# The update of x in a two-block transformer kernel: gain product in its own buffer, block 1 in two parts, last mean on VectorE

## The reference

```python
merged = concatenate([rms_norm(y_ssm, g_ssm), rms_norm(y_attn, g_attn)])
h = h + rms_norm(merged @ w_out, g_post_mix)       # the update of x
hn = rms_norm(h, g_pre_ffn)
gu = hn @ w_gate_up
ff = (silu(gu[..., :D_FF]) * gu[..., D_FF:]) @ w_down
return h + rms_norm(ff, g_post_ffn)                # the tail
```

## Time and profile before

| | us (the clock: a share) |
|---|---|
| median of 3 runs | 791.45 |
| lowest, highest run | 790.4, 792.85 |
| the profiled execution, its whole time | 792.52 |
| the profiled execution, span from first to last instruction | 790.7 |
| TensorE busy in the span | 775.4 |
| VectorE, ScalarE, GpSimd busy | 516.2, 405.2, 233.4 |
| TensorE's granted clock, mean, share of full speed | 0.998 |

### The profile page before, as it was taken

One profiled execution on the slowest core, in us unless ns is written; L12 is line 12 of the kernel. 1 busy time (PEld: TensorE's weight loads), 2 busy tenths in 40 slices (PEclk: granted clock), 3 DMA queues, 4 the chain that ended last, 5 costly groups with the idle time before them and its releaser, 6 DMA issues.

```text
span 790.7 us, 12717 instructions
## 1 busy us (share of the span) xinstructions
PE 775.4 (98%) x5139; PEld 678.8 (86%) x5139; DVE 516.2 (65%) x759; ACT 405.2 (51%) x649; POOL 233.4 (30%) x186
## 2 busy tenths in 40 slices
PE   8999999999999999999999999999999999999996
PEld 7889988999889889987778888989887888888885
DVE  4846884764547657866557965785678676777453
ACT  5644357534565545344335545717766555556341
POOL 3031896570742000036009910126002111011010
PEclk9999999999999999999999999999999999999999
DMA  9897996387621554655544556440363656654651
GB/s 229 200 240 203 219 221 172 84 196 170 164 81 53 188 173 147 214 165 146 159 143 148 183 200 188 134 134 2 133 220 121 198 183 212 186 183 167 222 177 54
DMA packets 78110, 130.72 MB, mean 165 GB/s; under 512 B 4447, under 2 KB 28243, under 8 KB 77923
## 3 DMA queue, kind: packets, MB, share of 16 engines
q1 hardware_dynamic: 76608, 124.96, 54.7%
q0 software_dynamic: 1200, 4.83, 1.9%
q10 hardware_dynamic: 242, 0.11, 0.1%
HBM read 128.82 MB, written 1.06 MB: 164 GB/s over the span
## 4 chain that ended last, share of the span: by engine, by line
PE 88%; DVE 4%; DMA 3%; ACT 3%; issue 1%; POOL 0%; DVEq 0%; SPq 0%; POOLq 0%; ACTq 0%
PE ps L1521 13%; PE ps L1525 13%; PE ps L1529 13%; PE ps L1561 10%; PE ps L1540 6%; PE ps L1544 6%; PE ps L1548 6%; PE ps L1565 5%; DMA stage<-in_even_w_in 3%; PE ps L1632 2%; PE ps L1651 2%; DVE w_lo L925 1%; ACT w_hi L636 1%; PE ps L1664 1%; PE ps L1663 1%
## 5 line engine op out<-in xcount | busy, mean ns | idle before, releaser
L925 DVE TENSOR_TENSOR w_lo<-stage,w_hi 128x1024 fp32r<-128x1024 f32 x226 | 299.6, 1346 | 161.9 <-ACT w_hi L636 161.3
L636 ACT ACTIVATE w_hi<-stage 128x1024 fp32r<-128x1024 f32 x232 | 242.2, 1061 | 240.0 <-PE ps L1529 106.6
L1521 PE MATMUL ps<-w_hi,act_t 128*128 128x512 f32 (+1 forms) x376 | 102.7, 395 | 4.0 <-issue 1.8
L1529 PE MATMUL ps<-w_lo,act_t 128*128 128x512 f32 (+1 forms) x376 | 98.8, 385 | 0.1
L1561 PE MATMUL ps<-act_t,w_hi 128*128 128x512 f32 x352 | 88.3, 393 | 0.7 <-DVE act_t L962 0.7
L1521 PEld LDWEIGHTS ps<-w_hi,act_t 128*128 128x128 f32 x376 | 67.9, 188 | 17.5 <-issue 2.8
L1529 PEld LDWEIGHTS ps<-w_lo,act_t 128*128 128x128 f32 x376 | 69.6, 188 | 14.8 <-DVE w_lo L925 0.5
L1525 PE MATMUL ps<-w_hi,act_t 128*128 128x512 f32 (+1 forms) x312 | 81.6, 384 | 0.0
L1561 PEld LDWEIGHTS ps<-act_t,w_hi 128*128 128x128 f32 x352 | 63.3, 189 | 12.2 <-issue 0.9
L1525 PEld LDWEIGHTS ps<-w_hi,act_t 128*128 128x128 f32 x312 | 57.6, 188 | 13.9 <-issue 2.0
L1540 PE MATMUL ps<-act_t,w_hi 128*128 128x256 f32 x416 | 58.9, 284 | 0.9 <-ACT w_hi L636 0.9
(11 more groups left out here) (364 smaller groups left out, 1197.2 us busy)
## 6 DMA issues: line engine op xcount, KB each, us to landing
stage<-in_even_w_in SPq DMA_DIRECT2D x64, 512.0 KB, 5.9
stage<-in_odd_w_in SPq DMA_DIRECT2D x48, 512.0 KB, 4.1
stage<-in_w_gate_up SPq DMA_DIRECT2D x44, 512.0 KB, 4.6
stage<-in_w_down SPq DMA_DIRECT2D x22, 512.0 KB, 4.1
stage<-in_even_w_out SPq DMA_DIRECT2D x16, 512.0 KB, 3.8
stage<-in_odd_w_out SPq DMA_DIRECT2D x16, 512.0 KB, 4.4
stage<-in_w_in SPq DMA_DIRECT2D x10, 512.0 KB, 4.5
stage<-in_w_out SPq DMA_DIRECT2D x8, 512.0 KB, 4.7
```

The source lines that it names most:

```text
L636: nc.scalar.activation(w_hi[:, u % RING, :], stage[:, u % RING, :], ACT.Copy).then_inc(hi_ready, 1)
L925: nc.vector.tensor_tensor(w_lo[:, u % RING, :], stage[:, u % RING, :], w_hi[:, u % RING, :].bitcast(F32), ALU.subtract).then_inc(lo_ready, 1)
L1521: mm(out[:, b, :], a_hi(k)[:, tok[b]], hi[:, i, :], start=(k == 0), stop=False)
L1529: ins = mm(out[:, b, :], a_hi(k)[:, tok[b]], lo[:, i, :], start=False, stop=(k == k_tiles - 1))
```

## The change

In words:

- `mix_gain(1, b)` writes to a new buffer `gained`, laid over a part of the work area that is no longer in use, and waits only for VectorE's own sum. `x_add(1, b)` reads `gained`.
- `mix_gain(1, 1)` moves ahead of `x_add(0, 0)`.
- `x_add(0, 1)` is made in two parts of 256 channels, each counting `x_ready` up; TensorE waits for the second part before tile 2 of block 1, and ScalarE for a count one higher.
- In the tail, VectorE adds the two halves' sums and epsilon (one instruction a block), and GpSimd only takes the power. So that the sums are means already, ScalarE's squares are scaled: those of half 0 by 1024 to the power -1/2, those of half 1 by `rstd_mean`, the factor times the same number, which VectorE makes once behind `spread`. ScalarE waits for it (`mean_ready`). The diff in full stands below.

```diff
@@ -181,7 +181,7 @@
         COL_LIM = COL_LRE + ST
         COL_FINAL = COL_LIM + ST
         sumsq, sumsq_b, rstd = sb("sumsq", [P, 18]), sb("sumsq_b", [P, 18]), sb("rstd", [P, 18])
-        rstd_in, rstd_in_q = sb("rstd_in", [P, NB]), sb("rstd_in_q", [P, NB])
+        rstd_in, rstd_in_q, rstd_mean = sb("rstd_in", [P, NB]), sb("rstd_in_q", [P, NB]), sb("rstd_mean", [P, NB])
         ones, diag = sb("ones", [P, P]), sb("diag", [P, NB, P])
         rstd_row, rstd_row_q = sb("rstd_row", [P, S]), sb("rstd_row_q", [P, S])
         neg_half, half_pi = sb("neg_half", [P, 8]), sb("half_pi", [P, 1])
@@ -236,6 +236,7 @@
         ssm_a, ssm_b = over("ssm_a", 8192, [P, CT, 2, 4, NC]), over("ssm_b", 10240, [P, CT, 2, 4, NC])
         y_ssm = [ssm_b[:, ct, 0].rearrange("p q n -> p (q n)") for ct in range(CT)]
         ssm_out, gate_z = over("ssm_out", 1024, [P, NB, 512]), over("gate_z", 2048, [P, NB, 512])
+        gained = over("gained", 8192, [P, NB, 512])
         rope_tmp = over("rope_tmp", 7168, [P, 768])
         ff_hi, ff_lo = over("ff_hi", 0, [P, KF, S], F32R), over("ff_lo", 5632, [P, KF, S], F32R)
         down_out, down_junk = (big[:, i * 2048:(i + 1) * 2048].rearrange("p (b n) -> p b n", b=NB) for i in range(2))
@@ -277,7 +278,7 @@
         b_pow_ready, c_pow_ready, lag_done, lag_copied, lag_ready, fade_ready = (sem(n) for n in ("b_pow_ready", "c_pow_ready", "lag_done", "lag_copied", "lag_ready", "fade_ready"))
         gelu_hi_ready, gelu_ready, gelu_lo_ready = sem("gelu_hi_ready"), sem("gelu_ready"), sem("gelu_lo_ready")
         rope_q_ready, rope_k_ready, k_out, qk_turned, qk_ready = (sem(n) for n in ("rope_q_ready", "rope_k_ready", "k_out", "qk_turned", "qk_ready"))
-        ret_stats = sem("ret_stats")
+        ret_stats, mean_ready = sem("ret_stats"), sem("mean_ready")
         sink_sum, sink_exped, y_attn_ready = sem("sink_sum"), sem("sink_exped"), sem("y_attn_ready")
         sig_ready, ssm_out_ready = sem("sig_ready"), sem("ssm_out_ready")
         ff_raw_ready, silu_ready, ff_ready, ff_hi_ready, ff_lo_ready, ff_part = sem("ff_raw_ready"), sem("silu_ready"), sem("ff_ready"), sem("ff_hi_ready"), sem("ff_lo_ready"), sem("ff_part")
@@ -617,10 +618,8 @@
             nc.gpsimd.tensor_tensor(down_out[:, :, 0:512], down_out[:, :, 0:512], row_b[:, 0:512].unsqueeze(1).to_broadcast([P, NB, 512]), ALU.mult).then_inc(down_scaled, 1)
             for b in range(NB):
                 c = slice(16 + b, 17 + b)
-                pool.wait_ge(block_squared, b + 1)
-                then(nc.gpsimd.tensor_tensor(sumsq[:, c], sumsq[:, c], sumsq_b[:, c], ALU.add))
-                then(nc.gpsimd.tensor_scalar(rstd[:, c], sumsq[:, c], 1.0 / D, EPS, ALU.mult, ALU.add))
-                nc.gpsimd.tensor_tensor(rstd[:, c], rstd[:, c], neg_half[:, 0:1], ALU.pow).then_inc(rstd_ready, 1)
+                pool.wait_ge(block_mean, NB + b + 1)
+                nc.gpsimd.tensor_tensor(rstd[:, c], sumsq[:, c], neg_half[:, 0:1], ALU.pow).then_inc(rstd_ready, 1)
 
 
         @block.scalar
@@ -879,7 +878,7 @@
                     nc.scalar.activation(junk[:, b, half], mixed[:, b, half], ACT.Square, scale=D**-0.5, accum_out=(sumsq, sumsq_b)[c][:, 12 + b:13 + b]).then_inc(squared, 1)
             ahead(("mix_ssm", 1))
             hi_of_turned(3 * KD + 24, KD, 0, COL_FFN)
-            act.wait_ge(x_ready, 2 * NB)
+            act.wait_ge(x_ready, 2 * NB + 1)
             squares(7, lambda b: x[:, b, :], lambda b: junk[:, b, :])
 
             def ff_hi_of(c):
@@ -905,11 +904,12 @@
             squares_half_down = lambda c, b, src, scale=1.0: nc.scalar.activation(down_junk[:, b, c * 512:(c + 1) * 512], src, ACT.Square, scale=scale,
                                                                                   accum_out=(sumsq, sumsq_b)[c][:, 16 + b:17 + b])
             for b in range(NB):
-                squares_half_down(0, b, down_out[:, b, 0:512]).then_inc(squared, 1)
+                squares_half_down(0, b, down_out[:, b, 0:512], D**-0.5).then_inc(squared, 1)
             ahead(("down", 1))
             for b in range(NB):
+                act.wait_ge(mean_ready, 1)
                 act.wait_ge(block_done, b + 1)
-                squares_half_down(1, b, result(("down", 1))[:, b, :], rstd[:, 14 + b:15 + b]).then_inc(block_squared, 1)
+                squares_half_down(1, b, result(("down", 1))[:, b, :], rstd_mean[:, b:b + 1]).then_inc(block_squared, 1)
 
 
         @block.vector
@@ -1365,8 +1365,11 @@
 
             def mix_gain(c, b):
 
-                dve.wait_ge(squared, squared_count(5) + 2 * c + b + 1)
-                return TT(mixed[:, b, halves[c]], mixed[:, b, halves[c]], row_a[:, halves[c]], ALU.mult)
+                if c == 0:
+                    dve.wait_ge(squared, squared_count(5) + b + 1)
+                    return TT(mixed[:, b, halves[0]], mixed[:, b, halves[0]], row_a[:, halves[0]], ALU.mult)
+                dve.wait_ge(mixed_ready, 2 + b + 1)
+                return TT(gained[:, b, :], mixed[:, b, halves[1]], row_a[:, halves[1]], ALU.mult)
 
             def mix_mean(b):
 
@@ -1374,10 +1377,14 @@
                 c = slice(12 + b, 13 + b)
                 STT(sumsq[:, c], sumsq[:, c], EPS, sumsq_b[:, c], ALU.add, ALU.add).then_inc(block_mean, 1)
 
-            def x_add(c, b):
+            def x_add(c, b, parts=1):
 
                 dve.wait_ge(rstd_ready, 7 + b)
-                STT(x[:, b, halves[c]], mixed[:, b, halves[c]], rstd[:, 12 + b:13 + b], x[:, b, halves[c]], ALU.mult, ALU.add).then_inc(x_ready, 1)
+                for part in range(parts):
+                    at = slice(part * (512 // parts), (part + 1) * (512 // parts))
+                    to = slice(c * 512 + at.start, c * 512 + at.stop)
+                    src = gained[:, b, at] if c == 1 else mixed[:, b, to]
+                    ins = STT(x[:, b, to], src, rstd[:, 12 + b:13 + b], x[:, b, to], ALU.mult, ALU.add).then_inc(x_ready, 1)
 
             ahead(("mix_ssm", 0))
             chunk_drained(dve, ("mix_attn", 0))
@@ -1393,14 +1400,14 @@
             mix_mean(0)
             chunk_done(dve, ("mix_ssm", 1))
             mix_sum(1, 1)
+            mix_gain(1, 1).then_inc(drain_sem(("mix_ssm", 1)), 1)
             chunk_drained(dve, ("mix_ssm", 0))
-            dve.wait_ge(mix_gained, 1)
             x_add(0, 0)
             mix_mean(1)
+            dve.wait_ge(mix_gained, 1)
             x_add(1, 0)
-            mix_gain(1, 1).then_inc(drain_sem(("mix_ssm", 1)), 1)
+            x_add(0, 1, 2)
             chunk_drained(dve, ("mix_ssm", 1))
-            x_add(0, 1)
             x_add(1, 1)
             lo_of_turned(3 * KD + 24, 4, 0, COL_FFN, KD)
             split_lo(next_unit[0] + 1)
@@ -1408,6 +1415,7 @@
             split_lo(last_unit[("ffn", 0)] + 1)
             dve.wait_ge(rstd_ready, 9)
             spread(rstd[:, 14:16])
+            TS(rstd_mean[:], rstd[:, 14:16], D**-0.5, None, ALU.mult).then_inc(mean_ready, 1)
 
             def ff_lo_of(c):
                 dve.wait_ge(ff_hi_ready, c + 1)
@@ -1433,6 +1441,8 @@
             dve.wait_ge(row_b_in, 32)
             for b in range(NB):
                 dve.wait_ge(block_squared, b + 1)
+                c = slice(16 + b, 17 + b)
+                STT(sumsq[:, c], sumsq[:, c], EPS, sumsq_b[:, c], ALU.add, ALU.add).then_inc(block_mean, 1)
                 then(STT(down_out[:, b, 512:1024], result(("down", 1))[:, b, :], rstd[:, 14 + b:15 + b], row_b[:, 512:1024], ALU.mult, ALU.mult))
                 dve.wait_ge(down_scaled, 1)
                 dve.wait_ge(rstd_ready, 10 + b)
@@ -1905,8 +1915,8 @@
             for b in range(NB):
                 keep_busy((6, 3)[b], (7, 0)[b])
                 for k in range(KD):
-                    if k % 4 == 0:
-                        pe.wait_ge(x_ready, 2 * b + k // 4 + 1)
+                    if k % 4 == 0 or (b, k) == (1, 2):
+                        pe.wait_ge(x_ready, (1, 1, 1, 1, 2, 2, 2, 2, 3, 3, 4, 4, 5, 5, 5, 5)[b * KD + k])
                     o = 4 * BANK + k * S + b * P
                     ins = nc.tensor.transpose(ps[:, o:o + P], x[:, b, k * P:(k + 1) * P], ident[:])
                     if b == 1:
```

## The result

The changed kernel took 794.59 us (median of 11 runs, 794.0 to 798.67) against 791.39 of the kernel before (median of 11, 789.81 to 793.57). The ratio is 1.0048, with a 95% interval of 1.0033 to 1.0062: slower by 3.2 us by the medians and 3.8 by the ratio, where 0.6 less was forecast, and outside the range that was given. The two places that the change edits did what was forecast, but for 0.06 us in the tail. The time was lost elsewhere, in matmuls that it does not touch.

A forecast was written before the change was run, and what follows sets the result against it. TensorE was busy 775.4 of 790.7 us, so only its pauses could be shortened. 0 (Part 1) + 0.26 (Part 2) + 0.36 (Part 3) = 0.62 us, from a median of 791.45 to 790.8 us; range 789.4 to 792.6.

The forecast's parts named there:

- Edits at nothing: Edits priced at 0: tail factor for the last square, ScalarE's wait for it, scales, x count, TensorE's extra wait, shifted buffers.
- rival C: Granted clock falls to 1.2 GHz between mixer and feed-forward part: 5.8 us more, 796.0 us; chance 0.02.
- the shifted addresses: Sign against the forecast: matmuls from 601 us on change their pace, through clock or shifted addresses; no size given.
- Part 1: Block 0's update of x between mixer and feed-forward: 0.61 us earlier, all spent on the moved gain product; gain 0.
- Part 2: Block 1's update of x between mixer and feed-forward: next transposes load 0.26 us earlier; ends 0 and 0.40.
- Rival A: Between the blocks' transposes, TensorE is not held by its warming matmuls: 0.40 + 0.36 = 0.76 us, 790.7; chance 0.10.
- the rule from the Trainium skill: VectorE with two SBUF inputs and GpSimd exclude each other: second power ends at 598.38, Part 2 is 0.24, not 0.26.
- Part 3: Tail after the down projection's last matmul: two GpSimd steps removed, one VectorE mean added; 0.36 us gained, ends 0.42 and -0.22.
- B: Between mixer and feed-forward, the moved gain product catches the first power: 0.16 slower, 791.6, or 0.74 slower, 792.2; chance 0.08.
- D: Between mixer and feed-forward, nothing gained because the second power comes later still: 0.36 alone, 791.1 us; chance 0.14.

The follow-up runs named there:

- e2: The kernel before with only an unused buffer of 32 bytes a partition in front of the work area: 795.49 us, ratio 1.0064.
- e8: e1 with block 1's gain product behind the two quarters and ScalarE's wait for the factor's mean ahead of its last loop: 790.21 us, ratio 0.9981.
- e7: e1 without the three warming matmuls between the two blocks' transposes: 791.26 us, one run.
- e1: The whole change, but rstd_mean takes the place of a buffer no longer in use, so no later buffer moves: 790.61 us, ratio 0.9992.
- e3: The kernel before with an unused buffer of 64 bytes a partition in front of the work area: 794.15 us, ratio 1.0044.
- e5: The kernel before with the work area moved by 128 bytes: 793.88 us, ratio 1.003.
- e6: The kernel before with w_lo moved 32 bytes past a multiple of 128 and all behind it moved by 128 bytes: 799.69 us, one run.

## Why the prediction was wrong

- **The step that failed** is in "Edits at nothing": "The new two-column buffer shifts all later buffers by 8 bytes; no row prices that, I take 0." The shift is 32 bytes, and it costs some 3.7 us (568 matmuls that start 6.5 ns further apart; e2, the shift alone, has ratio 1.0064), six times all the rest of the sum. No bound was given for it, so neither range nor rivals held it. (The rivals' 790.7 to 792.2 with 1 us either way would give 789.7 to 793.2, not 789.4 to 792.6, and rival C's own numbers give 796.6, not 796.0; the result lies outside either range.) It was named among the signs that would prove the forecast wrong ("or the shifted addresses"), and that is the one that came up.
- **Part 1**, all of block 0's 0.61 spent on the moved product: right. First update at 596.36 for 596.33, shown the other way round by e8.
- **Part 2**, 0.26: right, 10.80 to 10.54. Rival A fell: e7 gained 0.17 once the warming matmuls were gone. The second power took 1.00 beside the update with two SBUF inputs, and the first quarter waited 0.45 for it. By the rule from the Trainium skill, SBUF — State Buffer, "SBUF: two separate sides", it would have ended at 598.38; it ended at 598.26 on before's time, near the row's 598.22. The 0.12 between them did not decide anything here, since the warming matmuls held TensorE for longer.
- **Part 3**, 0.36: right from the square on. ScalarE's later start took 0.06 of it, so the tail gave 0.30. The prediction had called its new wait free because its event was long past.
- **Rivals B, C, D:** B did not occur (first power 0.57 long, ended at 596.41, before the product's start at 596.55). C did not: the granted clock was 1.00 in the seam. D did not: the second power kept its time to 0.04.
- **The sum** of what was priced, 0.62, came out as 0.26 + 0.30 = 0.56 in the changed kernel and 0.28 + 0.30 = 0.58 in e1. e1 is at 0.9992 of before, and 0.62 less than 791.39 is 0.9992 too. The interval, 0.9977 to 1.0008, holds no change as well, so the traces carry this, and that the ratios agree to the last digit is luck.

## What to carry to other kernels

A buffer that is added in the middle of the allocation moves all that lies behind it; before any such change is timed, print the addresses, and look at the mean time of matmuls that the change does not touch. Here the distance between a matmul's loaded and streamed operand, modulo 256 bytes, was by estimate worth six times the scheduling work. A new small buffer belongs into the place of a dead one, as in e1, or at the very end, which was not tried. And an instruction moved into a wait helps only if it is not put ahead of the next link: in e8, with the same instructions in another order, the seam was 0.38 us shorter.

## What the runs showed of the hardware

- float32r matmuls that stream 512 columns of a weight unit started 227 ns apart with loaded and streamed operand at equal places modulo 256 bytes a partition, and 231 to 234 apart with 32, 64, 96 or 128 bytes between them (groups of before against e2, e3, e5, e6; by the profile's modelled durations 389 against 394 to 396 in e2, e3 and e5). Matmuls of 256 columns did not show it (e6: 281 to 283 ns). The mean duration of the loads themselves stayed within 1 ns (187.8 before, 188.5 at most). Which part of TensorE or SBUF makes it so stays open, as do distances not tried.
- Two waits in a row ahead of a ScalarE instruction, the first long fulfilled, went with a later start: 0.10 us behind the last matmul's modelled end in the changed kernel, e1 and e7, and 0.04 in the kernel before and every other run. In e8, which has one wait there for block 1, it was 0.04 too (783.33 to 783.37).
- A GpSimd power of one column took 0.57 us beside a VectorE instruction with one input in PSUM, and 0.99 to 1.00 when it started some 0.16 into one with two SBUF inputs (before, changed kernel, e1, e7, e8).
